# One kernel, four layers: each token's gates spread by one product of 64 columns, norm sums made by VectorE, splits and maxima moved

## The reference, cut to what matters

```python
x = hgrn2_layer(x, ...)          # rmsnorm, x @ w_in, scan, x + o @ w_out        stages A, OA
k, v, F = shared_kv(x, ...)      # rmsnorm, x @ kv_w                             stages FG, F
x = fox_layer(x, ..., k, v, F)   # rmsnorm, attention with forget gate, x + o @ w_out   F, OF
x = x + mixed @ w_o              # rmsnorm, RG-LRU and sparse attention          X, C, OC
x = x + peer(rmsnorm_2(x, g), wq, keys1, keys2, u, v)                          # Q, U, V
return rmsnorm_2(x, g_final)

def rmsnorm(x, w):
    return x * lax.rsqrt(jnp.mean(x * x, axis=-1, keepdims=True) + EPS) * w

# peer, for 256 tokens: 8 heads x 16 experts each of 16384, by top_k of key scores
z = jnp.einsum('cd,ced->ce', xc, u[ec])
act = jax.nn.gelu(z, approximate=False) * gc
out = jnp.einsum('ce,ced->cd', act, v[ec])
```

## Time and profile before

| | |
|---|---|
| median of 3 runs | 3392.41 us (3392.05 to 3394.13) |
| profiled execution, its own time | 3395.45 us |
| its span | 3393.7 us |
| TensorE busy | 3323.1 us, 98% |
| VectorE busy | 2258.3 us, 67% |
| ScalarE busy | 1605.2 us, 47% |
| mean granted TensorE clock | 0.99 |

### The profile page before, as it was taken

The page is one execution under the profiler, slowest core; times in us unless marked ns, Lnnn a source line. Parts: engine busy times, 40 slices in busy tenths (PEclk is TensorE's granted clock), DMA queues, the critical chain, the costliest instruction groups (busy, mean ns, idle before and its releaser), DMA issues.

```text
span 3393.7 us, 64310 instructions
## 1 busy us (share of the span) xinstructions
PE 3323.1 (98%) x26164; PEld 3129.0 (92%) x26164; DVE 2258.3 (67%) x3620; ACT 1605.2 (47%) x2070; POOL 7.8 (0%) x27
## 2 busy tenths in 40 slices
PE   7999998999999999999999999999999999999998
PEld 7999998999999889999999999998899789987786
DVE  7767666544455565555558987875688557889755
ACT  5444454766673544555544434344433443344444
POOL 0000000000000000000000000000000000000000
PEclk9999999999999989999999999999999999999999
DMA  4444444444444435454545545455544554444454
GB/s 176 151 152 166 150 152 159 149 161 152 158 148 176 160 128 183 161 188 155 176 151 187 174 164 181 174 177 186 186 174 174 185 187 174 174 174 174 172 200 149
DMA packets 99066, 570.02 MB, mean 168 GB/s; under 512 B 9424, under 2 KB 30288, under 8 KB 31568
## 3 DMA queue, kind: packets, MB, share of 16 engines
q1 hardware_dynamic: 98896, 567.58, 47.2%
HBM read 565.45 MB, written 2.10 MB: 167 GB/s over the span
## 4 chain that ended last, share of the span: by engine, by line
PE 89%; DVE 7%; ACT 1%; DVEq 1%; DMA 1%; issue 1%; ACTq 0%; SPq 0%
PE bank L496 19%; PE bank L497 19%; PE bank L498 19%; PE bank L982 7%; PE bank L984 7%; PE bank L983 7%; DVE wl L1443 2%; PE bank L906 1%; PE bank L646 1%; PE bank L589 1%; PE bank L833 1%; PE bank L838 1%; PE bank L540 1%; ACT wh L1013 0%; PE bank L827 0%
## 5 line engine op out<-in xcount | busy, mean ns | idle before, releaser
L496 PE MATMUL bank<-hh,wh 128*128 128x256 f32 x5696 | 1626.3, 286 | 26.0 <-DVE wl L1443 11.1
L497 PE MATMUL bank<-hl,wh 128*128 128x256 f32 x5696 | 1592.1, 280 | 0.0
L498 PE MATMUL bank<-hh,wl 128*128 128x256 f32 x5696 | 1591.6, 279 | 0.0
L1443 DVE TENSOR_TENSOR wl<-raw,wh 128x1024 fp32r<-128x1024 f32 x1052 | 1253.4, 1221 | 503.3 <-ACT wh L1013 495.4
L1013 ACT ACTIVATE wh<-raw 128x1024 fp32r<-128x1024 f32 x1052 | 1051.2, 1049 | 347.7 <-DMA raw<-w_in_a 137.1
L496 PEld LDWEIGHTS bank<-hh,wh 128*128 128x128 f32 x5696 | 1078.3, 189 | 38.5 <-issue 16.7
L497 PEld LDWEIGHTS bank<-hl,wh 128*128 128x128 f32 x5696 | 1081.1, 190 | 8.3 <-issue 7.2
L498 PEld LDWEIGHTS bank<-hh,wl 128*128 128x128 f32 x5696 | 1082.4, 190 | 0.0
L982 PE MATMUL bank<-wh,ah 128*128 128x512 f32 x1024 | 407.9, 398 | 3.7 <-DVE al L2054 3.7
L984 PE MATMUL bank<-wl,ah 128*128 128x512 f32 x1024 | 404.8, 395 | 0.0
L983 PE MATMUL bank<-wh,al 128*128 128x512 f32 x1024 | 404.8, 395 | 0.0
(11 more groups left out here) (339 smaller groups left out, 2734.8 us busy)
## 6 DMA issues: line engine op xcount, KB each, us to landing
raw<-peer_u SPq DMA_DIRECT2D x128, 1024.0 KB, 4.8
raw<-peer_v SPq DMA_DIRECT2D x128, 1024.0 KB, 4.8
raw<-w_in_c SPq DMA_DIRECT2D x64, 1024.0 KB, 4.8
raw<-w_in_a SPq DMA_DIRECT2D x63, 1024.0 KB, 4.8
raw<-w_kv SPq DMA_DIRECT2D x32, 1024.0 KB, 4.8
raw<-w_in_b SPq DMA_DIRECT2D x32, 1024.0 KB, 4.8
raw<-w_out_a SPq DMA_DIRECT2D x16, 1024.0 KB, 4.8
raw<-w_out_b SPq DMA_DIRECT2D x16, 1024.0 KB, 4.8
```

The source lines that it names most:

```text
L496: eng.matmul(out, h_[:, k, :], high[:, k, :], start=(k == 0), stop=False)
L497: eng.matmul(out, h_[:, k, :], low[:, k, :], start=False, stop=False)
L498: last = eng.matmul(out, low_rows(c, k), high[:, k, :], start=False, stop=(k == KC - 1))
L1443: eng.tensor_tensor(low_half_out(c, half), raw_half(c, half), high_half(c, half).bitcast(F32), ALU.subtract).then_inc(lo_ready, 1)
```

## The change

- The two f16 products of a token become one: the weights are the same, the 64 columns are `gates_b`'s high and low half. The two results lie side by side in PSUM. ScalarE copies the low ones, scaled, to `g_low`; VectorE adds the high ones to them (`g_sum`), and multiplies `act` by the sum.
- The squares are added up by VectorE in `sq`, and TensorE sums them over the partitions by two matmuls per norm, the first over chunks 0 to 14 and the second over the last. Around them are matmuls of ones by ones into bank 7 that nobody reads (`keep_clock`): 3 between the two, 15 after them, and 14 after the sums of the first norm, which otherwise stay.
- Unit 3 after the first norm is split between the two passes by ScalarE and VectorE.
- In stage C the maxima of the softmax stand before the split of unit 7.
- Routing takes nine halves a head, and U0's products use banks 1 and 2 and no longer wait for the scores.
- Some small tiles lie elsewhere in SBUF and two of them are larger (`nmax_f`, `rsum_f`, `rinv_f`, `fsum`, `frstd`).

```diff
-ROUTE_UNITS = 4
+ROUTE_HALVES = 9
-DOT_BANK = (4, 4, 2, 0)
+DOT_BANK = (1, 4, 2, 0)
...
+        def gate_sums(c, part):
+            return B[6 + c % 2][:, :].rearrange("p (t g b) -> p g b t", g=2, b=BJ)[:, part]
...
+            def keep_clock(count):
+                for _ in range(count):
+                    eng.matmul(B[7][:, 0:P], ones[:, :], ones[:, :], start=True, stop=True)
...
+            def norm_sum(name):
+                eng.wait_ge(sq_summed, NORM_AT[name])
+                eng.matmul(B[4][:, 0:T], ones[:, :], sq[:, 0, 0:T], start=True, stop=False)
+                keep_clock(3)
+                eng.wait_ge(sq_ready, 8 * NORM_AT[name] + 8)
+                eng.matmul(B[4][:, 0:T], ones[:, :], sq[:, 1, T:2 * T], start=False, stop=True).then_inc(ss_done, 1)
+                keep_clock(15)
...
-                    if g >= 1:
-                        norm_sum(name, g - 1)
-                norm_sum(name, KC // 2 - 1)
+                norm_sum(name)
...
                 for t in range(TG):
-                    for g in range(2):
-                        last = eng.matmul(B[6 + c % 2][:, t * BJ:(t + 1) * BJ], hot_a[c % 2][:, t, :], gates_b[c % 2][:, t, g, :],
-                                          start=(g == 0), stop=(g == 1))
+                    last = eng.matmul(B[6 + c % 2][:, 2 * t * BJ:2 * (t + 1) * BJ], hot_a[c % 2][:, t, :],
+                                      gates_b[c % 2][:, t, :, :].rearrange("p g b -> p (g b)"), start=True, stop=True)
...
-                        if b == 0 and c < 2 and isinstance(i, int) and i == 0:
-                            eng.wait_ge(s["sc_ready"], PEER_HEADS - 1 + c)
...
             def square_chunks(name, g):
+                if g >= 2:
+                    eng.wait_ge(sq_added, 6 * (NORM_AT[name] - 1) + g - 1)
...
-                        if n == 1 and g == 6:
-                            high_part(0, NORM_UNIT[name] + 3)
...
                     if n == 0 and name != "A":
                         high_part(0, NORM_UNIT[name] + 2)
+                        if name == "F":
+                            high_part(0, NORM_UNIT[name] + 3)
...
+            def keep_low_gates(b, i, c):
+                n = i * PER_PAIR + (b * BJ + c)
+                eng.wait_ge(s["g_done"], n + 1)
+                if past_zero(n - 1):
+                    eng.wait_ge(s["gated"], n - 1)
+                eng.activation(g_low[c % 2][:, :, :], gate_sums(c, 1), ACT.Copy, scale=1.0 / G_SCALE).then_inc(s["g_low_ready"], 1)
...
             def gelus(b, i):
                 for c in range(PER_PAIR):
                     last_turn = isinstance(i, int) and i > 0
+                    if b >= 1:
+                        keep_low_gates(b - 1, i, c)
...
                 for n in range(BJ):
+                    if b == BLOCKS - 2:
+                        keep_low_gates(b + 1, 0, n)
                     if n + 2 < BJ:
                         act_high(b, (n + 2) // (BJ // 2), (n + 2) % (BJ // 2))
...
+                    if g >= 2:
+                        eng.wait_ge(sq_ready, 8 * NORM_AT[name] + g)
+                        eng.tensor_tensor(sq[:, 0, :], sq[:, 0, :], sq[:, 1, :], ALU.add).then_inc(sq_added, 1)
                     if g == KC // 2 - 1:
+                        eng.drain()
+                        eng.tensor_tensor(sq[:, 0, 0:T], sq[:, 0, 0:T], sq[:, 0, T:2 * T], ALU.add)
...
+                            if j == 0:
+                                eng.drain()
+                                eng.wait_ge(sq_next_to_last, NORM_AT[name])
+                                eng.tensor_tensor(sq[:, 0, 0:T], sq[:, 0, 0:T], sq[:, 1, 0:T], ALU.add).then_inc(sq_summed, 1)
...
+                softmax_maxima(s, i, prob_c, nmax_c, selmask)
                 low_part(i, u + 7)
-                softmax_maxima(s, i, prob_c, nmax_c, selmask)
                 softmax_weights(s, i, prob_c, rsum_c, rinv_c)
...
                 n = i * PER_PAIR + (b * BJ + c)
-                eng.wait_ge(s["g_done"], n + 1)
+                eng.wait_ge(s["g_low_ready"], n + 1)
+                part = acts[b % 2][:, :, ds(i * (PER_PAIR * TG) + c * TG, TG)]
+                eng.scalar_tensor_tensor(out=g_sum[c % 2][:, :, :], in0=gate_sums(c, 0), scalar=1.0 / G_SCALE, in1=g_low[c % 2][:, :, :],
+                                         op0=ALU.mult, op1=ALU.add)
                 if after is not None and rows_first:
                     hot_rows(*after)
-                part = acts[b % 2][:, :, ds(i * (PER_PAIR * TG) + c * TG, TG)]
-                eng.scalar_tensor_tensor(out=part, in0=B[6 + c % 2][:, 0:T].rearrange("p (t b) -> p b t", b=BJ), scalar=1.0 / G_SCALE,
-                                         in1=part, op0=ALU.mult, op1=ALU.mult).then_inc(s["gated"], 1)
+                eng.drain()
+                eng.tensor_tensor(part, g_sum[c % 2][:, :, :], part, ALU.mult).then_inc(s["gated"], 1)
```

More of the change, by code:

```diff
@@ L313, in program @@
         gT = sb_in(m, "gT", [P, T, 2], F16)
-        fsum = sb_in(m, "fsum", [P, NT, 4])
-        frstd = sb_in(m, "frstd", [P, NT])
+        g_low = [sb_in(m, f"g_low{n}", [P, BJ, TG]) for n in range(2)]
+        g_sum = [sb_in(m, f"g_sum{n}", [P, BJ, TG]) for n in range(2)]
         m.close()
@@ L2027, in gate @@
                         hot_rows(*after)
-                    eng.drain()
+                        eng.drain()
                     gate_rows(*after)
@@ L2102, in _ @@
             gate_distances()
-            for c in range(ROUTE_FIRST + ROUTE_UNITS * PEER_HEADS, BASE["U1"]):
+            for c in range(ROUTE_FIRST + ROUTE_HALVES * PEER_HEADS // 2, BASE["U1"]):
                 low_part(0, c)
```

51 lines of the change are left out of this document (28 added, 23 removed).

## The result

| | before | after |
|---|---|---|
| median, beside each other | 3392.61 us (3392.05 to 3394.13) | 3308.71 us (3302.48 to 3311.85) |
| ratio of the times | | 0.975, 95% interval 0.9733 to 0.9767 |
| span of the profiled execution | 3393.7 us | 3305.1 us |
| mean granted TensorE clock | 0.990 | 0.994 |

The change makes the kernel 83.9 us faster, 2.5%. The prediction was 53 us faster, 3339 us, with a range of 3320 to 3362.

What follows compares the result with a forecast made beforehand. TensorE, busy 98% of the span, was taken as the bound. The terms 20 (spread and gate, net) + 18 - 0.5 + 3.4 - 1 + 4 + 9.5 gave 53 us saved, a median of 3339 us, range 3320 to 3362.

Steps and rivals of the forecast that it cites:

- spread, 128 turns: Gated turns: 8 matmuls of 64 columns at 29 ns replace 16 of 32, 0.17 us a turn, 22 us saved.
- entries into V: Three changes from U to V: the gate's sum, drain and product and the shorter turn lengthen the `al` wait, 2 us lost.
- norm sums: Three output stages: seven of eight pairs of ones-matmuls leave TensorE in each, 0.87 us a pair, 18 us saved.
- clock behind two norms: After the second and third norm: added matmuls keep TensorE at full clock, 3.4 us gained.
- start of stage F: After the first norm: moving unit 3's split only shifts TensorE's wait one unit later; 1 us loss, bounds +1 and -3.
- attention: First attention pair of stage C: earlier maxima shorten the `prob_c` wait and low clock; 4 us gained, bounds 2 and 5.4.
- routing: Routing stage: nine halves and the other bank remove waits and clock loss; 9.5 us gained, bounds 5 and 11.
- What no part names: Units of 48 products alternate between two lengths in U turns, cause unknown; counted nothing, 10 us either way in range, chance 0.08.
- (a): Rival on the spread: columns add to the pitch, 40 ns a matmul, 3349 us; chance 0.12, 0.03 of it at 50 ns.
- (b): Rival: VectorE becomes the bound in gated turns, 0.1 or 0.4 us a turn over 32 turns, up to 3352 us; chance 0.10.
- (c): Rival: the hand-over to ScalarE stalls all 128 turns; at 2 us a turn 73 us slower than before, 3465; chance 0.03.
- (d): Rival: dummies and moved splits do nothing, clock still falls, routing and attention keep half their waits; 3349 us; chance 0.12.

Runs made afterwards that it cites:

- e12: Kernel after with the norm sums as before: matmul pairs between the products, without VectorE's additions; 3322.9 us, ratio 0.9789.
- e8: Kernel after with an empty `keep_clock`, so without its idle matmuls; 3310.3 us, ratio 0.9753.
- e16: Kernel after with the split of the second stage's fourth weight unit back behind the first norm's second pass; 3306.7 us, ratio 0.9753.
- e18: Kernel after with all tiles from `hh` on 64 bytes higher and the fourth weight unit's split back in its old place; 3310.3 us, ratio 0.9758.
- e17: Kernel after with the old order of the attention maxima, eight routing halves a head and the old bank for U0; 3320.4 us, ratio 0.9792.
- e3: Kernel before with only the new spread and gate; 3364.7 us, ratio 0.9914.
- e4: Kernel after with the old spread of 16 matmuls and the old gate, all else kept; 3337.1 us, ratio 0.9836.
- e15: Kernel after with each of the spread's eight products issued twice into the same place; 3337.5 us, ratio 0.9843.
- e1: Kernel after with `fsum` and `frstd` back in their old places, so `ah` and `al` lie 192 bytes lower; 3324.8 us, ratio 0.979.
- e2: Kernel before with only `fsum` and `frstd` moved ahead of `ah`; 3371.5 us, ratio 0.9934.
- e13: Kernel after with `eps` ahead of `hh`, so `hh` and `hl` begin 32 bytes below the weight tiles modulo 256; 3369.5 us, ratio 0.9936.
- e9: Kernel after with 64 bytes ahead of `hh`, moving it and all tiles behind it up together; 3303.7 us, ratio 0.9737.
- e5: Kernel after with `eps` and `qw` ahead of `hh`, so only `hh` and `hl` begin 64 bytes higher; 3395.1 us, ratio 1.001.
- e14: Kernel after with 32 bytes behind `qw`, so `hh` and `hl` begin 96 bytes below the weight tiles modulo 256; 3367.1 us, ratio 0.9926.

## Why the prediction was wrong

| term | predicted us | measured us | by |
|---|---|---|---|
| spread, 128 turns | 22 | 0.17 x 128 = 22 | burst 0.24 for 0.41 us |
| entries into V | -2 | -2.6 | wait for `al` 3.7 to 6.3 |
| norm sums | 18 | 13 by the times, 17 in the trace | e12 |
| end of the sum | -0.5 | not seen apart | |
| clock behind two norms | 3.4 | 3.8 in the trace, 1.5 by the times | e8 |
| start of stage F | -1 | -2.2 in the traces | e16, e18 |
| attention | 4 | 3.8 | e17 |
| routing | 9.5 | 8 | e17 |
| h products short | 0, 10 kept | 17.5, of them 11 in U turns | lengths; for the U turns e3, e4, e15 |
| V products short | 0 | 19 by the lengths, 14 and 22 by the times | e1, e2 |
| products of `kh` and `kl` short | 0 | 3 by the lengths | cause not shown |

**The step that failed** is in "What no part names": "The small tiles moved in SBUF are counted at nothing: no engine's work on them changes." No engine's work on them does change; they moved their neighbours. `ah` and `al` went from 0 to 192 bytes past a multiple of 256, which is where the weight tiles lie, and each of 3072 V products became 6 ns shorter. By the lengths that is 19 us, more than attention, routing and clock together, and it is what took the time out of the range: with `fsum` and `frstd` in their old places the kernel takes 3324.8 us (e1), inside of 3320 to 3362. I had read the diff for what each tile does and not for where the ones declared behind it land.

The rest was named in its main part. The prediction saw the two lengths in the earlier trace rows, worked out that 96 units on one side make 10 us, and put it in the range with a chance of 0.08 and no sign. All did fall on the short side, 11 us. e3, e4 and e15 show that this comes with the new spread and gate; why is open, so the step could not have been given a sign from the rows. Outside of the U turns the h products gave 6 us more, which the range had no room for and whose cause is open.

**The rest of the sum held.** Its terms came to 48 us by the third column (with 15 for the norms, and the traces' value for the clock and for stage F) where 53 were forecast. With 17.5, 19 and 3 us for the products that makes 87, against the 84 measured; the parts overlap a little, since some 4 us of e12's 17 are lengths of h products. Three smaller slips changed nothing. The waits of TensorE in the kernel before add up to 59 us and not to 50. The lower end of the range, 3320, is 9 us below the 3329 that the forecast less 10 us for the units gives, and no sentence says for what. The third is in the next paragraph.

The choice on the spread was the largest single decision: 29 ns a matmul and not 40 or 50, because the f32 rows show a weight load that hides the columns. The trace has eight in 0.25 us. The 70 cycles for 64 columns that the Trainium skill gives (VectorE: DVE Perf Modes, the table of engine clocks in its section on the TRN2 errata) are 29 ns, and the trace agrees. The Trainium skill's figure of 81 ns at 128 columns (TensorE: Matmul & The Clock Gate, Back-to-back issue gap) led the prediction to an estimate of 50 ns at 64 columns and to no saving. A straight line from 25 ns at 32 columns to that figure gives 44 ns at 64, by this estimate a saving of some 0.05 us a turn; neither is borne out by the 30 ns here.

**The rivals.** (a), the columns add to the pitch: refuted, 30 ns. (b), VectorE becomes the bound in V2: the turn is 5.82 us, and the list of waits has none of TensorE between 3000 and 3110 us. The margin was as thin as forecast: VectorE no longer idles at its two waits of the earlier trace rows and is busy for 167.49 of 170 us. (c), the hand-over stalls all turns: none does. (d), dummies and moved splits do nothing: routing and attention gave 12 us by e17, and the clock came back, though the time of e8 is too near to that of the kernel after to show it; the moved split in stage F costs 2 us.

**The entries into V.** TensorE waits 1.7 us at the longest, where it waited 1.4, and 6.3 in all: the sum, the drain and the shorter turn are in front of `ah` as forecast.

## What to carry to other kernels

When a diff moves, adds or resizes a tile, work out where every tile declared behind it begins, and compare moving with stationary tiles modulo 256 bytes; 32 bytes moved `hh` off its good place and cost 61 us here (e13), more than any change of order gave. Before and after any change count the matmuls in a stretch that it does not touch, at full clock and without waits: if the count differs, the change has a part that is in no line of its logic. And when a trace shows two lengths for the same code, run one kernel to find what sets them before predicting anything that stands between those units.

## What the runs showed of the hardware that was not expected

- A sustained f32 product depends on where its two operands begin relative to each other. h products: 114.3 ns at best, 119.9 at worst (e9, e5); V products: 227.2 and 233.3 ns (after, before). With nothing but 64 bytes between e5 and the kernel after, the time went from 3308.7 to 3395.1 us. That the partner is the other operand, and not what ScalarE and VectorE write beside it, is argued.
- It is the distance and not the place: with all tiles 64 bytes higher nothing changed (e9). The good distance isn't the same for the two kinds: 64 below for the h products, 0 for the V products, and 32 bytes beside the good one is already long (e13, e14). Only steps of 64 were run for V, and whether the period is 256 or 512 bytes was not run.
- At the best distance of the h products there are still two lengths, 113.3 and 117.7 ns, and in the U turns the small f16 matmuls between the units choose between them, by their form or by the gate that comes with it (e4 and e15: as many matmuls, in 0.42 and 0.48 us, and the products are all short only with the new form and gate). What does it, and whether the two effects have one cause, is open.
